# A two-block transformer layer on one core: the first projection as three rounded passes, with the norm's factor put on its outputs

## The reference, cut to what matters

```python
h = rms_norm(x, g_mix[l])          # x * rsqrt(mean(x*x) + eps) * g, over 2048 columns
proj = h @ w_in[l]                 # 60 column tiles of 128 in the kernel
p_dsa, p_rwkv = proj[..., :DSA_COLS], proj[..., DSA_COLS:]
q, k, v, q_idx, k_idx, w_idx = split_cols(p_dsa, DSA_SPLITS)
y_dsa = dsa_mixer(q, k, v, q_idx, k_idx, w_idx, q_gain[l], k_gain[l])   # norm, rope, top-k attention
p_rwkv = token_shift_mix(p_rwkv, rwkv_shift_mix[l])                     # p + (prev - p) * mu
r, d_w, kr, vr, d_a, d_g = split_cols(p_rwkv, RWKV_SPLITS)
y_rwkv = rwkv7_mixer(r, d_w, kr, vr, d_a, d_g, ...)                     # 16 heads, a scan over time
x = x + concatenate([y_dsa, y_rwkv]) @ w_out[l]
```

## Time and profile before

| | |
|---|---|
| median of 3 runs | 3280.18 us (3279.99 to 3282.33) |
| profiled execution, own time | 3280.27 us |
| its span | 3278.5 us |
| PE, DVE, ACT busy in the span | 96%, 57%, 42% |
| mean granted PE clock | 0.981 |
| start, up to the end of unit 5 | 0 to about 62 us |
| eight pairs | about 62 to 676 us |
| attention's norm, rope, index scores | 676 to about 768 us |

### The profile page before, as it was taken

The page is one execution under the profiler, slowest core; times in us unless marked ns, Lnnn a source line. Parts: engine busy times, 40 slices in busy tenths (PEclk is TensorE's granted clock), DMA queues, the critical chain, the costliest instruction groups (busy, mean ns, idle before and its releaser), DMA issues.

```text
span 3278.5 us, 46085 instructions
## 1 busy us (share of the span) xinstructions
PE 3156.5 (96%) x18702; PEld 2715.4 (83%) x18702; DVE 1855.9 (57%) x2416; ACT 1390.9 (42%) x1951; POOL 211.1 (6%) x263
## 2 busy tenths in 40 slices
PE   8999999998989999999998889999999999999998
PEld 7777777765768888777897779999998989889896
DVE  3333333356477787878657883444565555545454
ACT  2222222244456666656440014775444434434343
POOL 0000000020000000000157620000000000000000
PEclk9999999999989999999998998999999999999999
DMA  6222222211358888788453333445555555555554
GB/s 238 86 78 78 88 79 78 84 71 68 129 228 312 318 324 327 299 305 326 165 187 109 116 117 128 169 162 181 217 184 186 196 192 188 185 190 185 190 190 145
DMA packets 81782, 581.66 MB, mean 177 GB/s; under 512 B 9009, under 2 KB 9265, under 8 KB 12338
## 3 DMA queue, kind: packets, MB, share of 16 engines
q1 hardware_dynamic: 78912, 566.27, 47.3%
q10 hardware_dynamic: 2674, 12.54, 1.0%
HBM read 574.58 MB, written 4.19 MB: 177 GB/s over the span
## 4 chain that ended last, share of the span: by engine, by line
PE 84%; DVE 10%; ACT 2%; POOL 2%; issue 1%; DMA 0%; ACTq 0%; SPq 0%; DVEq 0%; POOLq 0%
PE PG L810 10%; PE PG L750 8%; PE PG L748 8%; PE PG L751 8%; PE PG L776 5%; PE PG L775 5%; PE PG L774 5%; PE PG L1129 4%; PE PG L1130 4%; PE PG L1131 4%; PE PX L880 3%; PE PG L719 2%; DVE work L2370 2%; DVE ring_r L637 1%; PE PX L1181 1%
## 5 line engine op out<-in xcount | busy, mean ns | idle before, releaser
L637 DVE TENSOR_TENSOR ring_r<-ring,work_r 128x1024 fp32r<-128x1024 f32 x468 | 553.9, 1226 | 325.0 <-ACT work_r L630 321.5
L630 ACT ACTIVATE work_r<-ring 128x1024 fp32r<-128x1024 f32 x468 | 469.3, 1052 | 488.4 <-PE PG L751 236.0
L810 PE MATMUL PG<-HT,ring 128*128 128x256 f32 x1728 | 435.1, 389 | 0.0
L637 DVE TENSOR_TENSOR ring_r<-ring,C_r 128x1024 fp32r<-128x1024 f32 x244 | 289.3, 1227 | 222.8 <-ACT C_r L630 219.4
L630 ACT ACTIVATE C_r<-ring 128x1024 fp32r<-128x1024 f32 x244 | 244.9, 1051 | 374.2 <-PE PG L751 253.7
L751 PE MATMUL PG<-work_r,ring_r 128*128 128x256 f32 x1344 | 373.3, 278 | 0.0
L751 PE MATMUL PG<-YT_r,ring_r 128*128 128x256 f32 x1280 | 361.4, 282 | 0.0
L810 PEld LDWEIGHTS PG<-HT,ring 128*128 128x128 f32 x1728 | 311.3, 190 | 55.4 <-issue 10.6
L751 PEld LDWEIGHTS PG<-work_r,ring_r 128*128 128x128 f32 x1344 | 254.5, 189 | 0.0
L775 PE MATMUL PG<-ring_r,HT_r 128*128 128x512 f32 x640 | 252.2, 394 | 0.0
L751 PEld LDWEIGHTS PG<-YT_r,ring_r 128*128 128x128 f32 x1280 | 244.8, 191 | 0.0
(11 more groups left out here) (592 smaller groups left out, 6389.3 us busy)
## 6 DMA issues: line engine op xcount, KB each, us to landing
ring<-weights SPq DMA_DIRECT2D x472, 1024.0 KB, 4.8
C<-weights SPq DMA_DIRECT2D x32, 1024.0 KB, 4.8
work<-weights SPq DMA_DIRECT2D x32, 1024.0 KB, 5.1
XT<-xT SPq DMA_DIRECT2D x4, 512.0 KB, 6.1
XT<-x ACTq DMA_DIRECT2D x1, 2048.0 KB, 9.4
residual<-XT ACTq DMA_DIRECT2D x4, 512.0 KB, 3.0
XT<-residual ACTq DMA_DIRECT2D x1, 2048.0 KB, 10.0
result<-YT SPq DMA_DIRECT2D x8, 256.0 KB, 4.1
```

The source lines that it names most:

```text
L630: act.activation(w_high(u)[:, c], weights(u)[:, c], ACT.Copy).then_inc(w_hi, 1)
L637: dve.tensor_tensor(w_low(u)[:, c], weights(u)[:, c], w_high(u)[:, c].bitcast(F32), ALU.subtract).then_inc(w_lo, 1)
L810: mm = pe.matmul(PG[:, u % BANKS, 0:T], ring[:, u % RING, k * P:k * P + P], HT[:, k, :], start=(k == 0), stop=(k == KT - 1))
```

## The change

What it does:

- All 60 units of the first projection are multiplied in three passes. ACT writes the high part of each half unit (`half_high`) to one of four places, DVE the low part (`half_low`) into the ring's slot. Behind half h of the weights the conversion of half h+4 follows, at places given by two tables, `ACT_HALVES` and `DVE_HALVES`.
- x is not normed ahead of the projection: ACT writes g*x rounded, DVE what the rounding left. The norm's factor RS is multiplied on the outputs: DVE takes every unit out of PSUM with RS (`with_factor`, `take_dsa`; before, ACT took the dsa tiles), the values tiles get it as a scale when ACT copies them, after a transpose of RS (two more transposes).
- SP loads the vectors, weight unit 0, then x, then units 1 to 3. The load of x by tokens moves from the start to behind the index scores.
- In a pair the three exponentials move ahead of the reciprocal root, a dummy Ln of one column is put ahead of each Ln, and the second reciprocal moves behind "kmax". PE's "lora" waits for the pair before's "var", not its "out".
- In attention, the last units' halves are converted at listed rounds: on DVE ahead of rope rounds 5, 9, 13, 17 and 21, on ACT behind its logarithms and exponentials.

```diff
+ACT_HALVES = {"tok": (0, 1), "sco": (2,), "sq2": (3,), "sq4": (4,), "t16": (5,), "W0": (6,), "W2": (7,), "W3": (8,),
+              "Z3": (9,), "gn2": (10,), "end": (11,)}
+DVE_HALVES = {"tok": (0, 1), "sco": (2,), "sq4": (3,), "sq8": (4,), "t16": (5,), "Z0": (6,), "Z2": (7,), "Z3": (8,),
+              "gn1": (9,), "next": (10, 11)}
...
+        def half_high(act, h):
+            u, c = h // 2, slice(h % 2 * (UNIT // 2), (h % 2 + 1) * (UNIT // 2))
+            act.wait_ge(slot_full[u % RING], 16 * (u // RING + 1))
+            if h >= 4:
+                act.wait_ge(unit_done if h % 2 else half_done, u - 1)
+            act.activation(high_half(h), ring[:, u % RING, c], ACT.Copy).then_inc(w_hi, 1)
+
+        def half_low(eng, h):
+            u, c = h // 2, slice(h % 2 * (UNIT // 2), (h % 2 + 1) * (UNIT // 2))
+            eng.wait_ge(w_hi, h + 1)
+            eng.tensor_tensor(ring_r[:, u % RING, c], ring[:, u % RING, c], high_half(h).bitcast(F32),
+                              ALU.subtract).then_inc(w_lo, 1)
...
             def product(u, k):
 
+                h = 2 * u + k // (KT // 2)
+                if k % (KT // 2) == 0:
+                    pe.wait_ge(w_lo, h + 1)
...
-                mm = pe.matmul(PG[:, u % BANKS, 0:T], ring[:, u % RING, k * P:k * P + P], HT[:, k, :],
-                               start=(k == 0), stop=(k == KT - 1))
+                pe.matmul(o, wh, HT_r[:, k, :], start=(k == 0), stop=False, skip_group_check=True)
+                pe.matmul(o, wh, XT_r[:, k, :], start=False, stop=False, skip_group_check=True)
+                mm = pe.matmul(o, wl, HT_r[:, k, :], start=False, stop=(k == KT - 1), skip_group_check=True)
...
+            products(0)
+            products(1)
+            pe.wait_ge(s_zero, 1)
+            pe.wait_ge(s_pairs, 3)
+            for n in range(4):
+                mm = pe.matmul(PX[:, 0, 0:T], ONES, X0SQ[:, 0, n * T:n * T + T], start=(n == 0), stop=(n == 3))
+            mm.then_inc(s_squsd, 1)
+            products(2)
...
-                    pe.wait_ge(DR.sem, DR.at(p - 1, "out"))
+                    pe.wait_ge(DR.sem, DR.at(p - 1, "var"))
...
+            half_high(act, 0)
+            half_high(act, 1)
+            for k in range(KT):
+                act.wait_ge(s_x[k // 4], 16)
+                act.activation(HT_r[:, k, :], X0[:, k, :], ACT.Copy, scale=vec("g_mix", k)).then_inc(x_tiles, 1)
+            half_high(act, 2)
+            half_high(act, 3)
...
                 for q in range(3):
+                    half_high(act, 2 * (V_UNIT + 2 + q))
+                    half_high(act, 2 * (V_UNIT + 2 + q) + 1)
                     take_v(q)
...
+            def with_factor(what):
+
+                m, u = MIX_ORDER.index(what), P1_AT[what]
+                dve.wait_ge(unit_done, u + 1)
+                dve.tensor_tensor(MBF[:, m % 3, 1:T + 1], PG[:, u % BANKS, 0:T], RS[:, :], ALU.mult) \
+                   .then_inc(free_bank(u), 1)
...
+                late = dict(zip((5, 9, 13, 17, 21), range(2 * V_UNIT + 4, HALVES)))
                 for r in range(25):
+                    if r in late:
+                        half_low(dve, late[r])
```

More of the change, by code:

```diff
@@ L601, in split_count, with high_half, after_half @@
         def split_count(u):
-            return u - U0["wo"] if u < U0["p2"] + S5_FIRST else u - U0["wo"] - (S5_END - S5_FIRST)
+            return u if u < U0["p2"] + S5_FIRST else u - (S5_END - S5_FIRST)
+        def high_half(h):
+            if h % 4 < 2:
+                return yt_r[:, h % 4 * (UNIT // 2):(h % 4 + 1) * (UNIT // 2)]
+            if h % 4 == 2:
+                return rounded_floats(WORK - UNIT // 2, UNIT // 2)
+            return rounded_floats(6 * PIECE, UNIT // 2) if h // 2 >= V_UNIT else sq_r
+        HALVES = 2 * U0["wo"]
+        FIRST_FILL = 2 * (P1_AT[("v", 0)] + 1)
+        DSA_TAKEN = P1_AT[("dsa", 24)]
+        def half_high(act, h):
[9 more added lines that the diff above has]
+                              ALU.subtract).then_inc(w_lo, 1)
+        def after_half(p, j):
+            h = 2 * (P1_AT[("v", p)] + 1) + j
+            return P1_ORDER[h // 2] if h % 2 else None, h // 2, h + 4
+        for p in range(MT):
+            ends = filler_ends(p)[1]
+            for table in (ACT_HALVES, DVE_HALVES):
+                assert sum(table.values(), ()) == tuple(range(len(ends)))
+                assert all(name not in PE_RW or ends[j] < PE_RW.index(name) for name in table for j in table[name])
         def w_high(u):
@@ L709, in _, with unit @@
         def _(pe):
-            def unit(u, use, x, kts=KT, tiles=1, first=None, full=0, free=0):
+            def unit(u, use, x, kts=KT, tiles=1, full=0, free=0):
                 pe.wait_ge(slot_full[slot(u)], 16 * loads(u) + full)
@@ L1459, in pair @@
                 done(act.activation(KK2, K_, ACT.Square, scale=vec("k_k", p)), "kk2")
+                dve("cum")
+                act.activation(PIN, CS, ACT.Exp, scale=-DECAY)
+                act.activation(PINV, CS, ACT.Exp, scale=DECAY)
+                done(act.activation(PPREV, CP, ACT.Exp, scale=-DECAY), "exps")
+                act.activation(SS[:, 3, 0, 0:1], con("ones")[:, 0:1], ACT.Ln)
                 dve("kmax")
@@ L1505, in pair @@
                 done(act.activation(YSQ, YC, ACT.Square), "ysq")
-                take_dsa("gn2")
+                act.activation(SS[:, 3, 0, 0:1], con("ones")[:, 0:1], ACT.Ln)
+                used_halves("gn2")
                 dve("var")
@@ L1509, in pair @@
                 done(act.activation(GRS, GRS, ACT.Exp, scale=-0.5), "grs")
-                while taken_[0] < len(ends):
-                    d = sum(DSA_PER_PAIR[:p]) + taken_[0]
-                    u = P1_AT[("dsa", d)]
-                    act.wait_ge(unit_done, u + 1)
-                    act.activation(DQ[:, d, :], PG[:, u % BANKS, 0:T], ACT.Copy).then_inc(free_bank(u), 1)
-                    taken_[0] += 1
+                used_halves("end")
             for p in range(MT):
@@ L1915, in _ @@
             dve.tensor_scalar(LO[0:32, 2, :], LO[0:32, 2, :], 0.5, 0.5, ALU.mult, ALU.add).then_inc(s_lo_dve, 1)
+            for h in range(10, FIRST_FILL + 3):
+                half_low(dve, h)
+                if h >= 10 and h % 2:
+                    with_factor(("rkv"[(h - 11) // 2], 0)) if h < FIRST_FILL + 3 else None
+            with_factor(("v", 0))
             def pair(p):
@@ L2012, in pair @@
                 done(dve.tensor_tensor(YT[:, MT + p, :], YC, G_, ALU.mult), "out")
+                if p + 1 < MT:
+                    with_factor(("v", p + 1))
+                else:
+                    used_halves("next")
             for p in range(MT):
```

279 lines of the change are left out of this document (165 added, 114 removed).

## The result

The changed kernel takes 3305.70 us, median of 4 executions (3298.84 to 3308.75), against 3280.09 us (3278.05 to 3282.33) for the kernel before: a ratio of 1.0075, with a 95% interval of 1.0062 to 1.0089. It is 25.6 us slower where 3269 us was forecast, so the time lies outside the range of 3248 to 3286, on the side that had 12 in 100. The profiled execution took 3308.75 us, of which its span is 3307.0.

A forecast was written before the change was run, and what follows sets the result against it. PE (busy 96%) bounds the kernel, but in the pairs a chain over three engines limits the gain. 3280.27 - 13.2 (start) - 12.7 (pairs) + 14.4 (attention) = 3268.8, predicted 3269 us, range 3248 to 3286.

The forecast's parts named there:

- the side that had 12 in 100: Whole kernel: the chance given to a time slower than 3286.8 us, 0.12.
- The step that failed: Attention, behind the rope: score rounds and bare products at PE's pace win 3.7 us, 0.6 of it spent on transposes and copy.
- From the output projection on both traces should run alike.: Stages from the output projection to the end: no difference between the kernels before and after.
- the forecast gain of 11 us: Whole kernel: 13.2 us won at the start, 12.7 in the pairs, 14.4 lost in attention, 3280.27 to 3268.8.
- Price of a product: First projection on PE: a three-pass product costs 0.352 to 0.364 us, against 0.432 now.
- Start: Units 0 to 5: PE begins at 10.8 us, unit 5 ends at 48.8 instead of 61.96, 13.2 us gained.
- Between the pairs: From one pair to the next: PE waits 3.4 us for "tilde"; "tok" starts 0.8 us earlier, of 4.1 to be had.
- The clock in the pairs: Behind most waits for "tilde" the granted clock drops, 1.25 us each, 1.8 at most; a pair gains 1.2 instead of 2.5.
- Attention up to the rope's end: Rope: DVE stands at round 5, 13.5 us late; low halves add 4.5; 17.5 late at the end.
- the rival by that rule: Pairs: each table switch adds a drain of about 1.38 us, some 10 us in all, about 3278; 2 in 100.
- The one on the slow side: Middle of the pairs: clock drops of 1.7 us behind two short waits each, 27 us, 3296; 10 in 100.
- the price of a fall from one place alone: Pairs: at 597 us eight products took 5.32 us instead of 3.5, so a clock drop cost 1.8 us.

The follow-up runs named there:

- Experiments 1: Changed kernel with the 14 bare products put between the rope's end and the 32 score rounds instead of behind them: 3281.93 us, ratio 1.0006.
- experiment 4: Changed kernel with only four of the 14 bare products put between the rope and the score rounds: 3279.48 us, ratio 0.9995.
- 9: Changed kernel with the three exponentials behind "rn" again and four bare products between rope and score rounds: 3268.26 us, ratio 0.9959.
- 3: Changed kernel with ACT's high half 2*V_UNIT+4 behind its first Ln and Exp group, unedited program profiled twice more: 3300.83 and 3274.51 us.
- experiment 11: Kernel before, unchanged, profiled a second time: 2479.4 us from last logit to end, against 2481.8 in its first profile and 2491.3 in the changed kernel's.
- experiment 10: Combined edits; its float32 profile: changed kernel, last six units in float32, exponentials behind "rn": 3246.49 to 3258.08 us six times, 3277.8 to 3281.2 four times.

## Why the prediction was wrong

**The step that failed** is the last sentence of the attention part: "The 32 score rounds and 14 bare products behind go at PE's pace: 46 x 0.08 = 3.7 back". It priced these rounds at the clock of the trace before. They ran at 1.2 GHz instead of 2.4: 23.6 us lost instead of 3.1 won, which is 26.7 of the 40.0 us between the forecast and this profile (36.7 by the medians). Experiments 1, 4 and 9 remove it by order alone, 3 shows it without any edit, and there, at full clock, the step's own price holds (2.8 won).

**A second term was put at nothing**: "From the output projection on both traces should run alike." Behind the last logit 9.5 us were lost in this profile. Its cause is open (experiment 11). With the clock held by experiment 4 the time is 3279.48, no faster than before and still 10.5 above the forecast; in its profile 6.0 of that lie behind the last logit. So the forecast gain of 11 us would not have come with the clock right either.

**Price of a product: right.** 15 products of unit 5 start 5.31 us apart (44.50 to 49.81), 0.354 each; 0.352 was used.

**Start: right in kind, 1.5 too much.** PE began at 11.71 instead of 10.8 and unit 5 ended at 50.3 instead of 48.8.

**Between the pairs: right.** PE waits 3.3 us for "tilde" (3.4 forecast). The three exponentials ahead of Ln were priced at 2.2 on the chain, too much; undoing them gave 7.2 us of wait back in seven pairs, 1.0 each, since DVE is the next bound.

**The clock in the pairs: right in kind.** The reciprocals that open the chain of pairs 0 to 3 in the changed kernel start at

```profile
53.79 1.75 DVE L2046 RECIPROCAL work<-work 128x256 f32<-128x256 f32 x1
128.06 1.75 DVE L2046 RECIPROCAL work<-work 128x256 f32<-128x256 f32 x1
202.33 1.75 DVE L2046 RECIPROCAL work<-work 128x256 f32<-128x256 f32 x1
279.16 1.75 DVE L2046 RECIPROCAL work<-work 128x256 f32<-128x256 f32 x1
```

74.27 us apart twice, with the clock at 1.00 behind the wait, then 76.83 and four times 75.5 with a fall: 1.2 us for a usual fall where 1.25 was forecast, and 2.6 for two of the six. Pairs together won 10.5 instead of 12.7. The missing 2.2 are all in pair 0: the first "out" starts at 123.4 instead of 138.0 us, a lead of 14.6, so pair 0 won 2.9 where 5 was forecast, and the seven behind it 7.6 where 7.7 was forecast. Why pair 0 won less was not taken apart. That a wait brings a fall is not regular in the kernel before either: its profile ahead of the change had one, the second profile (experiment 11) has two, 0.66 over 447 to 452 us and 0.58 over 526 to 530.

**Attention up to the rope's end: right.** Round 5 ends 32.8 us behind "out" (33.1 forecast), and the rope loses 17.9 (17.5).

**The rule on table loads.** In the changed kernel the dummy starts at 207.65, 1.29 us after its load at 206.36. The Trainium skill ("ScalarE: Activation LUTs", "What ACT_TABLE_LOAD costs") adds a drain of 1.38 us to each switch; by the trace there is none on this chain, so the rival by that rule is out.

**The rivals.** The one on the slow side was a clock rival, but at the wrong place: it put falls of 1.7 us each in the middle of the pairs and needed twelve of them. None came there in the profile of the changed kernel. One fall at the rope's end cost more than all of those.

**What was in reach.** The trace of before had a fall that lasted: the logits ran at 0.50 from 778 to 790 us, with PE busy in 8.68 of these 12 us, and at 1.00 from 791 to 797, with 5.88 of 6 busy. The working took the price of a fall from one place alone, where 128-row products followed, and never asked what follows the rope, though it had counted two added transposes and ACT's copy into that very place. That the fall was likely there could not be read from the kernel before, whose 76 further executions all lie within 3275.86 to 3286.84 us.

## What to carry to other kernels

Price a fall of the clock by the work that follows it, not by the wait ahead of it: behind a wait of 3.3 us it cost 1.2 to 2.6 us in a pair, behind waits of 0.5 and 0.35 us some 26 us ahead of 32 light rounds. Where a change makes an engine other than PE set the pace, look for the first sparse place behind it and keep a few independent products for it; four of 96 were enough here, moved and not added. A stall behind a row of in-order work can move when one item is pulled forward, as here; then shorten the row.

## What the runs showed of the hardware

The granted clock stayed at 0.50 from 721 to 781 us while the profile has PE busy for 10.00 of each 10.00 us, in three-pass rounds, and from 692 to 758 us in the float32 rounds of experiment 10. It rose in the changed kernel only when the bare products came behind the rounds (0.61 over 781 to 782 us, 1.00 behind it). It held 1.00 through the very same rounds when it came to them at 1.00. Which of the two happens can differ between executions of one program: 3274.5 to 3277.2 and 3300.6 to 3307.3 us. What in the state of an execution decides it was not found. In the kernel before the same place has waits of 0.32 and 0.29 us and no such second group of times was seen in 76 executions.
